# Three edits to a 1-core transformer kernel: keys rotated in the joined step, first transfers on one queue, a weight cast on VectorE

## The reference

```
def hybrid_layer(x, ...):                      # block 1, layers 0 and 1
    h = rmsnorm(x, norm_g)                     # x * rsqrt(mean(x^2)) * gain
    aq, ak, av, az, buv, bz, cq, ck, cv, cz, gl = split_cols(h @ w_in)
    # branch A: 4 heads (here heads 0 to 3), two softmaxes each, subtracted; RMS norm; silu gate
    # branch B: gelu, layer norm, causal mixing over 128 tokens
    # branch C: 8 heads of 64 (here 4 pairs, "heads" 4 to 7), dilated windows in one masked softmax
    #   qc = partial_rope(cq); kc = partial_rope(ck)
    #   oc = softmax(qc kc^T + mask) vc;  yc = oc * silu(cz)
    merged = sum_n sigmoid(gl_n) * (y_n @ w_branch_n)
    return x + merged @ w_out
```

## Time and profile before

| | |
|---|---|
| median of 3 runs | 2323.68 us (2322.32 to 2325.24) |
| the profiled execution's own time | 2325.3 us |
| its span | 2323.5 us |
| TensorE, matmuls | busy 2308.4 us, 99% of the span |
| VectorE | busy 1481.2 us, 64% |
| ScalarE | busy 978.6 us, 42% |
| mean granted clock | 0.999 |

### The profile page before, as it was taken

The page is one execution under the profiler, slowest core; times in us unless marked ns, Lnnn a source line. Parts: engine busy times, 40 slices in busy tenths (PEclk is TensorE's granted clock), DMA queues, the critical chain, the costliest instruction groups (busy, mean ns, idle before and its releaser), DMA issues.

```text
span 2323.5 us, 30126 instructions
## 1 busy us (share of the span) xinstructions
PE 2308.4 (99%) x11442; PEld 1881.9 (81%) x11442; DVE 1481.2 (64%) x2781; ACT 978.6 (42%) x1811; POOL 0.2 (0%) x4
## 2 busy tenths in 40 slices
PE   9999999999999999999999999999999999999998
PEld 6888888888888878888877788888887768888887
DVE  6788763435478784444587668566567777658565
ACT  5356542223446553222567543232336764323222
POOL 0000000000000000000000000000000000000000
PEclk9999999999999999999999999999999999999999
DMA  4333334333243333233221133314313112422322
GB/s 167 107 105 105 104 96 112 92 99 100 84 117 109 97 103 114 93 100 117 65 88 55 56 127 102 127 55 145 118 37 97 55 46 100 145 82 91 127 64 99
DMA packets 74766, 226.84 MB, mean 98 GB/s; under 512 B 15296, under 2 KB 16192, under 8 KB 73856
## 3 DMA queue, kind: packets, MB, share of 16 engines
q1 hardware_dynamic: 74336, 224.14, 30.9%
q10 hardware_dynamic: 288, 0.79, 0.1%
HBM read 205.36 MB, written 2.10 MB: 89 GB/s over the span
## 4 chain that ended last, share of the span: by engine, by line
PE 96%; DVE 2%; ACT 1%; issue 0%; DMA 0%; DVEq 0%; SPq 0%
PE bank L590 25%; PE bank L592 25%; PE bank L591 25%; PE bank L2235 2%; PE bank L2237 2%; PE bank L2236 2%; PE bank L1310 2%; PE bank L2054 1%; PE bank L2013 1%; PE bank L1294 1%; PE bank L2038 1%; PE bank L524 1%; PE bank L1283 1%; PE bank L1281 1%; PE bank L2067 1%; PE bank L2096 0%
## 5 line engine op out<-in xcount | busy, mean ns | idle before, releaser
L590 PE MATMUL bank<-h_hi,w_hi 128*128 128x512 f32 x1984 | 784.7, 396 | 0.7 <-DVE sz L1769 0.3
L592 PE MATMUL bank<-h_lo,w_hi 128*128 128x512 f32 x1984 | 773.4, 390 | 0.0
L591 PE MATMUL bank<-h_hi,w_lo 128*128 128x512 f32 x1984 | 773.0, 390 | 0.0
L1157 DVE TENSOR_TENSOR w_lo<-raw_w,w_hi 128x1024 fp32r<-128x1024 f32 x314 | 378.9, 1221 | 97.4 <-ACT w_hi L1145 94.1
L590 PEld LDWEIGHTS bank<-h_hi,w_hi 128*128 128x128 f32 x1984 | 372.7, 188 | 82.5 <-issue 8.3
L592 PEld LDWEIGHTS bank<-h_lo,w_hi 128*128 128x128 f32 x1984 | 372.4, 188 | 79.8
L591 PEld LDWEIGHTS bank<-h_hi,w_lo 128*128 128x128 f32 x1984 | 372.9, 188 | 72.1
L1145 ACT ACTIVATE w_hi<-raw_w 128x1024 fp32r<-128x1024 f32 x314 | 327.6, 1054 | 159.5 <-DMA raw_w<-w_dram 159.1
L2472 ACT ACTIVATE nrm<-bank 128x512 f32<-128x512 f32 x44 | 26.4, 599 | 288.4 <-PE bank L592 288.4
L1611 ACT ACTIVATE ext<-bank 128x512 f32<-128x512 f32 x48 | 28.7, 598 | 274.3 <-PE bank L592 274.3
L1918 DVE TENSOR_TENSOR rope_a<-ext,bank 128x512 f32<-128x512 f32 x32 | 22.0, 688 | 165.8 <-PE bank L592 109.7
(11 more groups left out here) (372 smaller groups left out, 3504.6 us busy)
## 6 DMA issues: line engine op xcount, KB each, us to landing
raw_w<-w_dram SPq DMA_DIRECT2D x312, 512.0 KB, 3.6
down_raw<-w_dram SPq DMA_DIRECT2D x36, 512.0 KB, 4.5
extra_raw<-w_dram SPq DMA_DIRECT2D x10, 512.0 KB, 4.6
k_lo<-k_lo SPq DMA_DIRECT2D x32, 128.0 KB, 2.3
ln_row<-row_dram SPq DMA_DIRECT2D x4, 1024.0 KB, 6.6
last_raw<-w_dram SPq DMA_DIRECT2D x8, 512.0 KB, 4.6
rowp<-row_dram SPq DMA_DIRECT2D x2, 1024.0 KB, 11.9
rot_t<-raw_t SPq DMA_DIRECT2D x128, 16.0 KB
```

The costliest lines, as they stand in the source:

```text
L590: nc.tensor.matmul(dst, lh, rh, start=start, stop=False)
L591: nc.tensor.matmul(dst, ll, rh, start=False, stop=False)
L592: return nc.tensor.matmul(dst, lh, rl, start=False, stop=stop)
L1157: nc.vector.tensor_tensor(lo_of(u), raw_of(u), hi_of(u).bitcast(F32), ALU.subtract) \
```

## The change

**Transfers.** Block 0 of `x` was the one transfer that ScalarE's queue issued. It is now issued by SyncE, third, behind `const` and `colp` and ahead of weight unit 0.

**Gain.** `gain_diagonal` is one operation over 128x1024 where it was two over 128x512, and both sums wait for it. Ahead of the sums stand two full products of zeros, where it was one and a half. The product of zeros behind the sums is gone.

**Cast.** The high part of weight unit 1 is made by VectorE, ahead of `norm_half(1, 0)`, and no longer by ScalarE.

**Rotation.** In heads 4, 5 and 6 the next head's keys are rotated in step 1, right behind its queries, and no longer in step 2 behind the maxima.

```
             for tb in range(NB):
-                if tb:
-                    sp.dma_start(x[:, tb, :], x_in[tb * P:(tb + 1) * P, :]).then_inc(x_loaded[tb], 16)
+                sp.dma_start(x[:, tb, :], x_in[tb * P:(tb + 1) * P, :]).then_inc(x_loaded[tb], 16)
                 if tb < 2:
                     load(tb)
...
         def gain_sums(pe):
+            pe.wait_ge(gain_diag_ready, 1)
             for c in range(2):
-                pe.wait_ge(gain_diag_ready, c + 1)
...
-            for c in range(2):
-                nc.vector.tensor_tensor(gain_diag[:, 4 * c:4 * c + 4, :], ident.unsqueeze(1).to_broadcast([P, 4, P]),
...
+            nc.vector.tensor_tensor(gain_diag[:, :, :], ident.unsqueeze(1).to_broadcast([P, KD, P]),
...
-                zero_products(1)
-                zero_products(1, SEQ // 2)
+                zero_products(2)
                 pe.wait_ge(ident_loaded, 16)
                 gain_sums(pe)
-                zero_products(1)
...
-                act.dma_start(x[:, 0, :], x_in[0:P, :]).then_inc(x_loaded[0], 16)
...
-                cast_to(act, 1)
+                cast_units[0] = 2
...
             entry_lo(dve, e, 0, (0,))
+            dve.wait_ge(raw_loaded[TURN[1] % RAW], 16 * loaded_parts(1))
+            nc.vector.tensor_copy(hi_of(1), raw_of(1)).then_inc(hi_cast, 1)
             norm_half(1, 0)
...
+                    if qb == 2 and a in JOINED1 and a > N_A:
+                        dve.wait_ge(y_ready, at(y_ready, 3 + a))
+                        epilogue(a - 1, False)
+                    if qb in (1, 2) and a in JOINED1:
+                        normalise(a, qb)
+                    if before in ROTATE1 and not (a in JOINED1 and qb == 2):
+                        rotate(*ROTATE1[before])
                     if second1(a, qb):
-                        normalise(a, qb)
-                    if before in ROTATE1:
-                        rotate(*ROTATE1[before])
+                        rotate(*ROTATE1[a, qb])
                     if (a, qb) in EPILOGUE1:
                         if qb:
-                            dve.wait_ge(qk_ready, at(qk_ready, 2 * a + 3))
+                            dve.wait_ge(qk_ready, at(qk_ready, 2 * a + 4))
                         epilogue(EPILOGUE1[a, qb])
-                    elif qb == (2 if a in JOINED1 else 1) and a > N_A:
+                    elif qb == 1 and a > N_A and a not in JOINED1:
                         epilogue(a - 1, False)
```

More of the change, by code:

```diff
@@ L1171, in gain_diagonal @@
             dve.wait_ge(norm_loaded, 16)
-            for c in range(2):
-                nc.vector.tensor_tensor(gain_diag[:, 4 * c:4 * c + 4, :], ident.unsqueeze(1).to_broadcast([P, 4, P]),
-                                        colp[:, P1_NORM + 4 * c:P1_NORM + 4 * c + 4].unsqueeze(2).to_broadcast([P, 4, P]),
-                                        ALU.mult).then_inc(gain_diag_ready, 1)
+            nc.vector.tensor_tensor(gain_diag[:, :, :], ident.unsqueeze(1).to_broadcast([P, KD, P]),
+                                    colp[:, P1_NORM:P1_NORM + KD].unsqueeze(2).to_broadcast([P, KD, P]), ALU.mult) \
+              .then_inc(gain_diag_ready, 1)
         def tensor_block1(pe, layer):
@@ L1191, in tensor_block1, with zero_products @@
             if layer == 0:
-                def zero_products(n, cols=SEQ):
+                def zero_products(n):
                     for _ in range(n):
-                        nc.tensor.matmul(O[:, 0:cols], ytmp[:, 0:P], ytmp[:, 0:cols], start=True, stop=True)
+                        nc.tensor.matmul(O[:, :], ytmp[:, 0:P], ytmp[:, :], start=True, stop=True)
                 pe.wait_ge(zeros_ready, 1)
-                zero_products(1)
-                zero_products(1, SEQ // 2)
+                zero_products(2)
                 pe.wait_ge(ident_loaded, 16)
                 gain_sums(pe)
-                zero_products(1)
                 entry_transpose(pe, e, 0, hn[0], (0,))
@@ L1420, in scalar_block1 @@
             at, n0, e = Counts(names, layer), layer * B1_UNITS, ENTRY1[layer]
-            if layer == 0:
-                act.dma_start(x[:, 0, :], x_in[0:P, :]).then_inc(x_loaded[0], 16)
             nc.scalar.preload_act_table_set("natural_log_exp_and_others")
@@ L1904, in vector_block1 @@
                         dve.wait_ge(y_ready, at(y_ready, 4 + a))
-                    if not second1(a, qb):
+                    if qb not in (1, 2) or a not in JOINED1:
                         normalise(a, qb)
```

## The result

| | before | after |
|---|---|---|
| median of 13 runs | 2324.17 us | 2327.98 us |
| range of the runs | 2322.32 to 2325.24 | 2325.47 to 2329.59 |
| profiled execution: span | 2323.5 | 2327.8 |

The changed kernel takes 3.8 us longer, a ratio of 1.0016 (95% interval 1.0008 to 1.0023). That is within 0.2%, as forecast, but clear of zero and above the range given, which ended at 2326.8. Both traces are of executions at the slow end of their 13: 2329.59 us after, 1.6 above the median, and 2325.24 before, 1.1 above it. Stages are read from the traces, and what an edit is worth from the medians.

A forecast was written before the change was run, and what follows sets the result against it. TensorE, its matmuls busy 99% of the span, was taken as the bound, so only its idle time counts. Terms -2.5 (entry), -0.2 (cast), +3.1 (rotation) sum to +0.4 on 2323.68, giving 2324.1 us; range 2321.0 to 2326.8.

The forecast's parts named there:

- the price of the rotation: Head 5, both layers: a 3.04 us wait for maxima replaces 1.47 us of waits; +3.1 us, between +2.6 and +3.8.
- the rule on the clock: Entry: TensorE is clocked at 1.2 GHz until busy for a while, then 2.4; removing the gap brings the faster rate forward.
- The mechanism of the wait: Head 5: step 2's maxima are ready 4.28 us later, so TensorE's scores stand 3.04 us later; the 1.28 us wait goes.
- the slower rival: Head 5: the keys' rotation waits for its row swaps; at 4 us late the time is 2332; chance 0.04.
- The rival by which the wait of head 5 goes away: Head 5: the rotation removes the old wait, saving 2 x 1.47 us if bank `O` is freed early; 2318.1 us; chance 0.08.
- The entry: First 17 us: earlier transposes give -2.5 and the cast of unit 1 -0.2, together -2.7 us, between -0.2 and -3.6.
- the entry gives little: Entry: zero products still run slowly or `colp` lands no earlier, so it gives 0.7 us; time 2326.1; chance 0.15.
- The sum: Whole kernel: -2.5 - 0.2 + 3.1 = +0.4 us, giving 2324.1 us; the forecast as worked out had chance 0.73.

The follow-up runs named there:

- e2_entry: The changed kernel with the rotation of all heads put back, so only the three entry edits: 2321.57 us, -2.4 against the kernel before.
- e4_heads_4_6: The changed kernel with head 5 in the order of before; heads 4 and 6 still rotate the keys early: 2321.09 us, -2.8 against before.
- e1_rotation: The kernel before with the rotation edit alone, entry as before: 2328.75 us, +4.8 against before.
- e3_rotation_busy: The kernel before with the rotation edit and 12 unread products ahead of head 5's step 3 scores, in both layers: 2327.34 us, +3.4 against before.
- e10_changed_busy: The changed kernel with 12 unread products ahead of head 5's step 3 scores, in both layers: 2325.10 us, +1.1 against before.
- e9_epilogue_first: Three entry edits, rotation of before, head 3's epilogue moved ahead of the weight split in head 5, step 1: 2318.75 us, -5.2 against before.
- e7: The kernel before with the transfer edit alone: 2321.72 us, -2.4 against before.
- e11: The kernel before with the transfer edit and the gain and zero-product edit, without cast and rotation edits: 2322.20 us, -1.9 against before.
- e8_cast: The kernel before with the cast edit alone: 2324.54 us, +0.5 against before.

## Why the prediction was wrong

**The step that failed** is the price of the rotation, "The rotation costs 2 x 1.57 = +3.1 us", with the bound above it, "from above, with 0.3 us to start TensorE again in each, +3.8". Measured it was 6.2 to 6.6 us in the changed kernel (its +3.8 less the -2.4 of e2_entry or the -2.8 of e4_heads_4_6) and 4.8 alone. The price of a wait was taken to be its length. Behind a wait of nearly 3 us TensorE ran at its lower clock for several microseconds, and that has a price of its own: 3.8 - 1.1 = 2.7 us in two layers in the changed kernel's medians, and 4.2 and 2.5 us in the traces of that kernel and of e1_rotation. The text had named the rule on the clock in the entry, where TensorE comes out of idleness, and not in head 5, where the forecast itself put it back into it.

**What held.** The mechanism of the wait was the one forecast. The maxima became the wait, in head 5 of both layers and in no other. Its size was right too: each head 5 was to become 1.57 us longer, and with the wait filled it is 1.65 (e3_rotation_busy and e10_changed_busy). The values and transposes no longer waited. Heads 4 and 6 hid the edit (e4_heads_4_6). The keys' rotation didn't wait for its row swaps, so the slower rival is out. The rival by which the wait of head 5 goes away is out too: VectorE's work ahead of bank `O` is the same, and only taking work out of it helped (e9_epilogue_first). In the medians the rotation without the lower clock cost 3.4 and 3.5 us where 3.1 was forecast.

**The entry** was forecast as -2.7 and measured as -2.4. Sums at 5.0, transposes at 8.6 and the first product near 11 are in the trace as 5.02, 8.51 and 10.57. But the number is in part luck. The forecast gave the zero product behind the sums much weight; alone it and the single diagonal give 0.8 us, not clear of nothing, while the transfers alone give 2.4. The columns were in use at 3.19 and not at 3.5, and the sums took less than the 3.54 us assumed, so that TensorE waited 0.60 us for `hn` ahead of the transposes. And where the full rate happens to come early, as in e1_rotation, the entry of before has its first real product at 10.56, as early as the changed one. The rival "the entry gives little" is out.

**The sum.** The forecast was -2.7 + 3.1 = +0.4, and the medians have -2.4 + 3.5 + 2.7 = +3.8. (The parts are differences of the same medians, so that they add up proves nothing; the table of head 5 is the independent reading.) The smaller errors are 3.5 less 3.1 for the wait and 0.3 for the entry, together 0.7. The other 2.7 us is the lower clock, which the forecast didn't have. The range ended 1.2 us below the measured time because its upper end came from an entry that gives little and not from a dearer wait.

**A late transfer.** From about 1199 us on the trace after is another 0.5 us behind the trace before, in a stretch that none of the edits touches. The start of it is VectorE's wait for a row swap, before (first row) and after (second row):

```profile
1184.16 0.69 DVE L2633 TENSOR_TENSOR rope_a<-raw_t,cos 128x512 f32<-128x512 f32 x1 [0.61 <-DMA nrm<-raw_t]
1188.73 0.69 DVE L2634 TENSOR_TENSOR rope_a<-raw_t,cos 128x512 f32<-128x512 f32 x1 [1.44 <-DMA nrm<-raw_t]
```

VectorE is then some 0.8 us late, and TensorE's scores at 1199.23 wait for its maxima. The six traces that lose 0.5 us here (after, e1, e4, e7, e10, e11) have this wait at 1.4 us or more, e8_cast has 1.38 and loses 0.1, and the other six traces, with 0.2 to 0.7, lose nothing. So it doesn't follow the edits. Why the transfer lands late in some executions stays open.

## What to carry to other kernels

When a wait of TensorE is moved or lengthened, its price is not only its length: look at how long the engine stands in one piece, and read the granted clock behind it. Here waits of 1.3 us cost their length, and waits of 2.7 us cost between 1.1 and 2.6 us more than theirs in the traces.

A wait for a buffer that one engine reads out late is cured by taking work out of the run ahead of the read-out (here an epilogue moved into idle time, 2.8 us), and not by changing the order within it. Before moving an operation forward on a busy engine, list what it is moved past and who waits for each of those.

A small transfer that starts the chain should have nothing large issued ahead of it, on any queue. And an edit to the first microseconds is priced by medians: two traces of one and the same entry had their first real product 3 us apart.

## What the runs showed of the hardware

The moment at which TensorE gets its full rate at the start of a program is not set by the program alone. With the same entry, the two float32 sums took 3.75 us in one execution (the kernel before) and 1.96 us in another (e1_rotation), and the first real product started at 13.59 and at 10.56. The page's granted clock says 1.00 in these slices in both, so it has to be read from the durations there. The Trainium skill says so too: by "TensorE: Matmul & The Clock Gate", Part 1, the gate runs free of the kernel's start, and the transition comes at another place from run to run. These two traces agree, but they lie 3.0 us apart, and that section has some 500 ns to either side.

In the middle of the program TensorE stood for 2.71 to 2.73 us in four places (head 5 of both layers, in the changed kernel and in e1_rotation), and in all four the granted clock fell to its lower level during the wait or within 1 us of its end, with the products 0.43 us apart instead of 0.23. Behind the waits of 1.28 us in the kernel before it stayed at 1.00, and so it did where added products filled the wait.

The 4 KB of columns were in use 3.9 us after their issue (5.05 less 1.17) where 512 KB of `x` had been issued 0.43 us ahead of them on ScalarE's queue, and 2.0 us after it (3.19 less 1.18) where `x` was issued behind them on the same queue. From issue to landing they took 3.8 and 1.9 us, and the 128 KB of `const` issued ahead of them 3.5 and 2.2. Which of the two helped, the order or the common queue, no run separates. The Trainium skill, "DMA: Bandwidth & Descriptors", section "Issuing engines are not separate DMA queues", says that transfers started by different engines run on the same 16 DMA engines and interleave. The traces agree: moving `x` behind the columns sped them up, and cost `x` itself 0.7 us.
